# Gathering expert rows by plain f32 products, half a weight unit staged early, and four moves of small steps in a two-model transformer kernel

## The reference, cut to what matters

```python
def squared_relu_mlp(h, w1, w2):
    return jnp.square(jax.nn.relu(h @ w1)) @ w2

def ec_moe(h, w_router, w_gate, w_up, w_down):      # cap = 32 tokens of each expert
    logits = jnp.einsum('bsd,de->bse', h, w_router)
    aff = jax.nn.softmax(logits, axis=-1)
    top_val, top_idx = lax.top_k(aff.transpose(0, 2, 1), cap)
    xg = jax.vmap(lambda hb, ib: hb[ib])(h, top_idx)
    g = jnp.einsum('becd,edf->becf', xg, w_gate)
    u = jnp.einsum('becd,edf->becf', xg, w_up)
    y = jnp.einsum('becf,efd->becd', jax.nn.silu(g) * u, w_down) * top_val[..., None]
    return scatter_add(y, top_idx)
```

## Time and profile before

| | |
|---|---|
| median of 3 runs | 2306.1 us (2304.45 to 2307.54) |
| the profiled execution | 2316.15 us, span 2314.1 us |
| PE busy | 1975.1 us (85%), granted clock 0.94 in the mean |
| DVE, ACT busy | 913.9 us (39%), 621.4 us (27%) |
| DMA in the expert stretches | 426 GB/s, nine tenths busy or more in nearly every slice |

### The profile page before, as it was taken

How to read it: one execution, slowest core, us unless ns; L and a number is a source line. 1 busy time by engine, 2 the same in 40 slices (tenths; PEclk the granted TensorE clock), 3 DMA queues, 4 the chain that set the end, 5 groups by cost and what they waited for, 6 DMA issues and landing times.

```text
span 2314.1 us, 34736 instructions
## 1 busy us (share of the span) xinstructions
PE 1975.1 (85%) x14706; PEld 1371.2 (59%) x14706; DVE 913.9 (39%) x1636; ACT 621.4 (27%) x1067; POOL 32.9 (1%) x51
## 2 busy tenths in 40 slices
PE   8988999999998999999997666667999997666665
PEld 7776757888656887988854222223978854222222
DVE  4665645767554576544521000002544531000001
ACT  3332334431134443464410000001464420000000
POOL 0100000000000000000000000000000000000000
PEclk9999999999999999999999888878999999888888
DMA  9311125678863776542699999999642699999997
GB/s 326 126 38 39 39 82 216 250 263 294 306 230 133 253 256 223 183 145 104 245 403 424 426 426 426 426 426 408 222 141 90 244 409 426 426 426 426 427 427 314
DMA packets 150918, 641.93 MB, mean 277 GB/s; under 512 B 9406, under 2 KB 30936, under 8 KB 117654
## 3 DMA queue, kind: packets, MB, share of 16 engines
q1 hardware_dynamic: 144506, 637.13, 69.6%
q10 hardware_dynamic: 6300, 3.20, 0.5%
HBM read 639.21 MB, written 1.10 MB: 277 GB/s over the span
## 4 chain that ended last, share of the span: by engine, by line
PE 61%; DMA 29%; DVE 4%; ACT 3%; issue 2%; DVEq 1%; SPq 0%; POOL 0%; ACTq 0%; POOLq 0%
DMA ring<-in_w_down 29%; PE psum L1413 6%; PE psum L1028 5%; PE psum L1029 5%; PE psum L1030 5%; PE psum L1566 4%; PE psum L726 3%; PE psum L1132 3%; PE psum L1403 2%; PE psum L1541 2%; PE psum L1292 2%; PE psum L1291 2%; PE psum L1293 2%; PE psum L1149 1%; PE psum L797 1%
## 5 line engine op out<-in xcount | busy, mean ns | idle before, releaser
L1541 PE MATMUL psum<-ring,arena 128*32 128x256 f32 x3840 | 270.6, 434 | 156.8 <-DMA ring<-in_w_up 119.9
L1541 PEld LDWEIGHTS psum<-ring,arena 128*32 128x32 f32 x3840 | 135.1, 121 | 294.5 <-issue 129.5
L1566 PE MATMUL psum<-ring,arena 128*32 128x512 f32 x992 | 155.2, 759 | 79.9 <-DMA ring<-in_w_down 70.0
L1028 PE MATMUL psum<-arena_r 128*128 128x512 f32 x512 | 205.6, 402 | 12.2 <-DVE arena_r L2033 7.1
L2446 DVE TENSOR_TENSOR arena<-psum,arena 128x256 f32<-128x256 f32 x32 | 13.6, 425 | 501.9 <-PE psum L1541 501.9
L1030 PE MATMUL psum<-ring_r,arena_r 128*128 128x512 f32 x512 | 203.2, 397 | 0.0
L1701 DVE TENSOR_TENSOR ring_r<-ring,arena_r 128x2048 fp32r<-128x2048 f32 x64 | 143.7, 2288 | 86.9 <-ACT arena_r L2525 86.9
L2453 DVE TENSOR_TENSOR arena<-psum,arena 128x512 f32<-128x512 f32 x64 | 44.3, 692 | 249.6 <-PE psum L1566 248.0
L2525 ACT CAST arena_r<-ring 128x2048 fp32r<-128x2048 f32 x64 | 119.5, 1903 | 72.9 <-PE psum L1030 72.9
L2962 ACT ACTIVATE arena<-psum 128x256 f32<-128x256 f32 x32 | 12.3, 385 | 467.6 <-PE psum L1541 467.6
L1566 PEld LDWEIGHTS psum<-ring,arena 128*32 128x32 f32 x992 | 31.3, 125 | 171.5 <-DMA ring<-in_w_down 99.2
(11 more groups left out here) (429 smaller groups left out, 3348.5 us busy)
## 6 DMA issues: line engine op xcount, KB each, us to landing
ring<-in_w_down SPq DMA_DIRECT2D x62, 2048.0 KB, 26.1
ring<-in_w_gate SPq DMA_DIRECT2D x60, 2048.0 KB, 26.5
ring<-in_w_up SPq DMA_DIRECT2D x60, 2048.0 KB, 26.0
ring<-in_mlp_w SPq DMA_DIRECT2D x32, 2048.0 KB, 8.6
ring<-in_w_mod SPq DMA_DIRECT2D x24, 2048.0 KB, 11.1
ring<-in_w_in SPq DMA_DIRECT2D x20, 2048.0 KB, 8.2
ring<-in_gdn_w_in SPq DMA_DIRECT2D x8, 2048.0 KB, 13.8
ring<-in_dswa_w_in SPq DMA_DIRECT2D x9, 1536.0 KB, 13.2
```

The costliest lines, as they stand in the source:

```text
L1028: mm(o, xh, wh, start=start, stop=False, skip_group_check=True)
L1541: ins = mm(PS[32 * j:32 * j + 32, 4 + m, 0:T], XGF[:, k, 0:CAP] if first else XGE[:, k, :], row[:, j * T:(j + 1) * T], start=u == 0 and kk ...
L1566: ins = mm(PS[32 * j:32 * j + 32, (7, 4)[half], :], HTE[:, k % 2, 32 * (k // 2):32 * (k // 2) + 32], (next_row(4, j) if ahead else W(v + 4 ...
```

## The change

1. *Start.* PE no longer waits for the parameters first; it runs ten `keep_busy` products as soon as the zero tile is there.
2. *MLP.* `turn(0)` moves into `up(1,1)`, behind its second pair of rows. On ACT `square(0)` moves between the two halves of the down weights, ahead of `relu(1,1)`; on DVE `hidden_low(0)` moves between the two halves too.
3. *DSWA.* `mod_cols(7)` and its sum move from ahead of `out_steps(0)` to behind `weighted(5)`. Then come four steps of `out_steps(2)`, `mod_cols(8)`, and the other eight. On DVE `mod_sum(7)` stands directly ahead of `mod_sum(8)` and the two `low` of the next MLP.
4. *Router.* `keep_busy` products go between the transposes and the router products, whose order is cut finer.
5. *Gather.* `first_rows` and `gather` use the plain f32 rows XN and a plain f32 `ST`. The four parts are no longer made.
6. *Staging.* The room of `XNH_R` becomes `NEXT5`, half of expert 1's sixth unit. SP issues it, and two parts of `NEXT1`, between the up and the down units of expert 0. The ring's load of that unit shrinks to 1 MB.

```diff
-        XNH_R = ar_r[:, 0:TT * D].rearrange("p (t d) -> p t d", t=TT)
+        NEXT5 = ar[:, 0:2 * D]
...
+                    if between:
+                        between()
                     for u in range(max(first - 4, 0), 2):
-                        load(n + 4 + u, two(A["w_down_2"])[u * 512:(u + 1) * 512, :].rearrange("(j p r) n -> p j (r n)", p=P, r=2), turn)
+                        rows = two(A["w_down_2"])[u * 512 + (T if first else 0):(u + 1) * 512, :]
+                        load(n + 4 + u, rows.rearrange("(j p r) n -> p j (r n)", p=P, r=2), turn)
...
+                def free_rooms():
+                    sp.dma_start(NEXT5, down[512:512 + T, :].rearrange("(p r) n -> p (r n)", r=2)).then_inc(sem("next1_in"), 16)
+                    for part, ks in ((1, slice(6, 7)), (2, slice(7, 8))):
+                        sp.dma_start(NEXT1[part].rearrange("p (k n) -> p k n", n=D), second[:, ks, :]).then_inc(sem("next1_in"), 16)
+                expert(0, 0, 0, free_rooms)
...
-            pe.wait_ge(sem("params_in"), PARAMS)
             pe.wait_ge(sem("filled"), 1)
+            keep_busy(10, 0)
+            pe.wait_ge(sem("params_in"), PARAMS)
...
-                up(1, 1, 5)
-                turn(0)
+                up(1, 1, 5, lambda: turn(0))
...
-            mod_cols(7, 2)
-            pe.wait_ge(sem("mod_out"), 8)
+            pe.wait_ge(sem("mod_out"), 7)
             pe.wait_ge(sem("tok_out"), 6 + 4)
             out_steps(0, 0, 3)
...
             weighted(5)
+            mod_cols(7)
+            out_steps(2, 0, 4)
             mod_cols(8)
-            out_steps(2, 0, 12)
+            out_steps(2, 4, 12)
...
-                for t in range(TT):
-                    norm_split(L * 2 + 5, t, True)
-                    router(0, 6 * t, 6 + 2 * t)
+                keep_busy(2, 7)
+                norm_split(L * 2 + 5, 0, True)
+                keep_busy(2, 1)
+                router(0, 0, 2)
+                keep_busy(1, 1)
+                router(0, 2, 4)
+                keep_busy(1, 1)
+                norm_split(L * 2 + 5, 1, True)
+                router(0, 4, KC)
+                keep_busy(1, 1)
                 router(1, 0, KC).then_inc(sem("router_mm"), 1)
-                keep_busy(2, 1)
+                keep_busy(3, 1)
...
-                        for part in (XNH_R, XN_R):
-                            ins = mm(o, part[:, t, :].rearrange("p (q k) -> p k q", k=KC)[:, dc], ST_R[:, t, a:z],
-                                     start=t == 0 and part is XNH_R, stop=t == 1 and part is XN_R, skip_group_check=True)
+                        ins = mm(o, by_rows(t)[:, dc], ST[:, t, a:z], start=t == 0, stop=t == 1, skip_group_check=True)
...
+                    for t in range(TT):
+                        ins = mm(bank(5 + half), ST[:, t, 0:ROWS4], XN[:, t, half * 512:(half + 1) * 512], start=t == 0, stop=t == 1)
...
                 for u in range(NU):
-                    if u < NU - 1:
-                        low(l, down_unit(u))
-                    hidden_low(u)
+                    if u == 0:
+                        low(l, down_unit(0), (0,))
+                        hidden_low(0)
+                        low(l, down_unit(0), (1,))
...
-            mod_sum(7, 2)
...
             mod_unit(17)
+            mod_sum(7)
             mod_sum(8)
             low(1, 0)
...
-                high(l, down_unit(0))
+                high(l, down_unit(0), (0,))
+                square(0)
+                high(l, down_unit(0), (1,))
                 relu(1, 1)
-                square(0)
```

More of the change, by code:

```diff
@@ L389, in next_row @@
         def next_row(unit, kk):
+            if unit == 5:
+                return NEXT5[:, kk * D:(kk + 1) * D]
             if unit == 4:
@@ L554, in _, with expert @@
                     ld(V_OUT + u, halves(one(A["w_out_2"]), u))
-                def expert(e, first, ahead=AHEAD):
+                def expert(e, first, ahead=AHEAD, between=None):
                     n = u2 + V_MOE - ahead
@@ L564, in expert @@
                                 load(n + 2 * m + u, pmajor(two(A[name]))[:, 4 * u:4 * u + 4, :], turn)
+                    if between:
+                        between()
                     for u in range(max(first - 4, 0), 2):
-                        load(n + 4 + u, two(A["w_down_2"])[u * 512:(u + 1) * 512, :].rearrange("(j p r) n -> p j (r n)", p=P, r=2), turn)
+                        rows = two(A["w_down_2"])[u * 512 + (T if first else 0):(u + 1) * 512, :]
+                        load(n + 4 + u, rows.rearrange("(j p r) n -> p j (r n)", p=P, r=2), turn)
                 second = pmajor(one(A["w_gate_2"])[1])
                 sp.dma_start(NEXT2.rearrange("p (k n) -> p k n", n=D), pmajor(one(A["w_up_2"])[1])[:, 0:4, :]).then_inc(sem("next0_in"), 16)
-                expert(0, 0, 0)
+                down = one(A["w_down_2"])[1]
+                def free_rooms():
[3 more added lines that the diff above has]
+                expert(0, 0, 0, free_rooms)
                 sp.dma_start(NEXT0.rearrange("p (k n) -> p k n", n=D), second[:, 0:4, :]).then_inc(sem("next0_in"), 16)
-                for part, ks in ((1, slice(6, 7)), (2, slice(7, 8))):
-                    sp.dma_start(NEXT1[part].rearrange("p (k n) -> p k n", n=D), second[:, ks, :]).then_inc(sem("next1_in"), 16)
                 sp.wait_ge(sem("router_mm"), L + 1)
@@ L577, in _ @@
                 sp.wait_ge(sem("sel_mm"), L * 3 + 2)
-                down = one(A["w_down_2"])[1]
                 for part, room in enumerate((X[:].rearrange("p t d -> p (t d)"), NEXT4)):
@@ L1045, in up @@
                             ins = three(bank(b), HTH_R[:, k, ts], HT_R[:, k, ts], wh[:, c], wl[:, c], k == 0, k == KC - 1)
+                            if k == 1 and between:
+                                between()
                         if t == 1 and hf == 0:
@@ L1577, in expert @@
                     ins.then_inc(sem("expert_done"), 1)
-                def first_rows(half, part, t):
-                    return mm(bank(5 + half), ST_R[:, t, 0:ROWS4], part[:, t, half * 512:(half + 1) * 512],
-                              start=t == 0 and part is XNH_R, stop=t == 1 and part is XN_R, skip_group_check=True)
-                pe.wait_ge(sem("xn_hi"), L * 2 + 2)
-                pe.wait_ge(sem("st_ready"), L * 3 + 1)
+                pe.wait_ge(sem("st_ready"), L * 2 + 1)
                 for half in range(2):
@@ L1588, in _ @@
                         pe.wait_ge(sem("gr_out"), L * 2 + 2)
-                    first_rows(half, XNH_R, 0)
-                    first_rows(half, XN_R, 0)
-                    first_rows(half, XNH_R, 1)
-                pe.wait_ge(sem("st_ready"), L * 3 + 2)
-                for half in range(2):
-                    first_rows(half, XN_R, 1).then_inc(sem("xg_mm"), 1)
+                    for t in range(TT):
+                        ins = mm(bank(5 + half), ST[:, t, 0:ROWS4], XN[:, t, half * 512:(half + 1) * 512], start=t == 0, stop=t == 1)
+                    ins.then_inc(sem("xg_mm"), 1)
                 for half in range(2):
@@ L1693, in residual, with low @@
                         square_part(h)
-            def low(l, i):
-                for hf in range(2):
+            def low(l, i, hfs=(0, 1)):
+                for hf in hfs:
                     h, slot, at = 2 * i + hf, mlp_unit(l, i) % RING, slice(hf * HALF, (hf + 1) * HALF)
@@ L2035, in mlp @@
                 for u in range(NU):
-                    if u < NU - 1:
-                        low(l, down_unit(u))
-                    hidden_low(u)
+                    if u == 0:
+                        low(l, down_unit(0), (0,))
+                        hidden_low(0)
+                        low(l, down_unit(0), (1,))
+                    else:
+                        if u < NU - 1:
+                            low(l, down_unit(u))
+                        hidden_low(u)
                     if u < NU - 2:
@@ L2410, in _ @@
                 chosen(0, 4)
-                rows_low(1).then_inc(sem("st_ready"), 1)
                 def gathered(n, a, z, src):
@@ L2514, in norm, with high @@
                                  bias=0.0 if shift is None else shift(dc)).then_inc(sem("ht0_ready"), 1)
-            def high(l, i):
+            def high(l, i, hfs=(0, 1)):
                 full(act, mlp_unit(l, i))
-                for hf in range(2):
+                for hf in hfs:
                     h = 2 * i + hf
```

25 lines of the change are left out of this document (11 added, 14 removed).

## The result

The changed kernel takes 2294.8 us (median of 7 runs, 2290.3 to 2298.3) beside 2309.9 us for the kernel before on the same chip: a ratio of 0.993, 95% interval 0.9914 to 0.9946, or 12 to 20 us faster; the medians differ by 15.1 us. The forecast was 18.8 us. The profiled execution took 2290.3 us, the shortest of the seven, with a span of 2288.3. The two profiled executions differ by 25.9 us, almost eleven more than the medians, so a single pair of traces says too much; the table further down therefore sets fourteen traces side by side.

What follows compares the result with a forecast made beforehand. PE was taken to bound the kernel up to expert 0 of each layer, then the weight transfer. Terms 4.0 + 11.8 + 1.8 + 1.2 = 18.8 us; 2306.1 - 18.8 = 2287 us, range 2277 to 2299.

Steps and rivals of the forecast that it cites:

- The start: Ten zero products at the start bring transposes and decay products to the upper clock level: 4.0 us faster, ends 1.8 and 7.3.
- The MLPs: In both MLPs the wait before `down(0)` goes (3.5 us each) and the clock holds behind it: 11.8 us faster, lower end 7.1.
- The DSWA: Output products come 8.5 us better, 4.7 returned behind two sums, 2.0 to a new pause: 1.8 us faster, between 0 and 3.8.
- Router and first rows: Before expert 0, `first_rows` costs 1.6 us more and the router's clock gains 1.6: 0 a layer, between +1.3 and -4.6.
- Rival A: The clock falls in the router anyway, each layer losing 4.6 us: 2296 us, chance 0.14.
- Gather and staging: In the experts, 2.46 us fewer bytes a layer against a gather 4.2 us longer: -0.2 and +1.4, 1.2 us faster in sum.
- the hole: DMA dips some 60 us after the steady transfer begins, standing 2.7 and 1.1 us because of the longer gather.
- the forecast's own signs: Listed signs of right or wrong; wrong included waits elsewhere in the MLPs, a router at 0.50, or DMA that never dips.
- D: `gather` in the experts runs at the lower clock level, 24.0 us long: 5.3 us slower, 2311 us, chance 0.04.
- Rival C: The MLPs' waits come back because what moves behind the square makes the next weights late: 2294 us, chance 0.08.

Runs made afterwards that it cites:

- e2: The kernel before with only the ten zero products at the start added: 1.0013 of before, 2311.7 us.
- e0: The changed kernel run again unaltered, for a second profile: 0.9936 of before, 2295.1 us.
- e5: The changed kernel without the ten zero products at the start: 0.9933 of before, 2295.5 us.
- e1: The kernel before with only the MLPs' new order: 0.9955 of before, 2301.4 us.
- e6: The changed kernel with the second MLP's first low half on DVE moved between the two modulation sums: 0.9918 of before, 2291.3 us.
- e12: e11 with the router as in the kernel before, without zero products between its groups: 0.9922 of before, 2292.6 us.
- e11: The changed kernel with e6's move and the start's zero products as 128 records instead of 20: 0.9894 of before, 2287.3 us.
- e3: The kernel before with only the seventh set of modulation columns in the DSWA moved later: 0.9992 of before, 2310.0 us.
- e9: The changed kernel with many more short zero products at the start, meant as 128 records but shifting by 240: 0.9965 of before, 2301.1 us.

## Why the prediction was right, and where it was not

The time, the direction and most steps came out. Two terms were off, the start by some 4 us and the gather with the staging by some 3, in opposite directions, and nearly cancelled. That the sum fits so well is luck.

- **The start: 4.0 us, measured none.** This step failed. The local part was right: products at the upper level, chunk products from 15.3 instead of 20.15, 4.8 us on average at the first turn pause (70.8 us in the six kernels with 20 zero records, 75.6 in the five without). What the step left out is that twenty records more shift all that PE executes later against the blocks in which its instructions come. The forecast asked what the zero products delay and what they speed up, and did not ask what they move. The core is 5.4 us longer with them in the mean of the same kernels (221.6 and 216.2 us; 6.8 in e2 against before, 5.6 in e0 against e5): 3.0 us more of pauses, and a clock that is at the lower level for 17.1 to 23.9 us instead of 10.2 (20.5 in e3).
- **The MLPs: 11.8 us, measured 10.4 alone (6 to 15 by its interval) and 5.5 + 5.5 to 6.7 by stage.** Right with its parts, the wait and the clock behind it.
- **The DSWA: 1.8 us, measured 1.8 alone, in an interval that holds none, and 0 to 2.6 by stage.** Each part was right: the output products come 5.7 us sooner and run at 2.81 us, the low halves are behind two sums, the new pause is 3.76 us (3.6), and the second MLP starts at the lower level. Against e1, which has all of the MLPs' gain and no such pause, the second MLP takes 2.7 us more (2.0 were taken off). e6 shows that pause and clock have one cause: move the one line, and 5.2 us come back in the two stages.
- **Router and first rows: 0 a layer, measured 0 within a us.** The two parts of it are shown as well: without the zeros (e12 against e11) the clock falls for 10.2 and 6.8 us instead of 3.4 and 3.4, and expert 0 comes 3.2 and 0.8 us later (1.6 each were forecast). Rival A, the fall in the router, did not come in layer 0 of the changed kernel; in layer 1 it came for 3.4 us, and expert 0 was no later for it.
- **Gather and staging: 1.2 us, measured 3.9 alone, 4.4 by stage** (439.0 and 440.2 us in the mean of the four kernels without it, 436.7 and 438.1 in the eight with it and one gather). The bytes are worth what was said, the hole that was to eat them is the step that failed in size. By the forecast's own signs a DMA that never dips speaks against it, and it does not dip. In hand were 1.4 and 1.1 us, where the forecast came to 2.7 and 1.1 too few. The gather took 11.2 us and not 12.0, so 3.4 more and not 4.2; DMA moved 420 GB/s in that stretch and not 426, which is 0.9 us over 64. And in layer 0 the profiled execution before had its clock down behind the old gather, so that the load came 59.9 us behind the first, where e1, e2 and e3 have it at 58.6. That is 3.0 of the 4.1 us in layer 0 and 1.7 of 2.2 in layer 1; the rest stays open.
- **D, the gather at the lower level**, did not come: 1.00 throughout. Rival C fell with e1.

The eleven us by which the profiled pair exceeds the medians are in no term: the core and the expert stretches differ by some us between executions, also of one kernel (e0 and the first profile: 440.7 and 435.3 in the first layer's experts). In the core it is the time at the lower clock, as the stage table shows; why that differs with the same records (e11 and e12) stays open. In e0's experts the weights fall behind in the first 45 us of the steady transfer: its first load is issued 2.1 us later than in the first profile and lands 2.0 later, but from 1204 on they land some 5 us later, to the end. What held them up stays open too.

## What to carry to other kernels

Work that only keeps PE busy is not free because it lies in a wait: count its records, since in stretches of very short products it moves the places where PE runs out of instructions. A whole period of records leaves them where they were (e11, e12), if the added products do not themselves outrun the supply (e9). When an operation is moved later, look at the queue behind its consumer and put something useful between two waits; the move is worth its full gain only then. Take the room that a transfer has in hand from more than one execution, or measure it by doubling what it hides.

## What the runs showed of the hardware

- PE's records of 32x32 products come in blocks of 128 (127 of them in the trace), with pauses of 0.2 to 2.2 us between them that the profile puts down to issue; each of the 121 in the cores ends 1.2 to 1.7 us after a packet of 16384 bytes has landed on the queue that the page calls "instruction". Inserting 20, 110 + 18 or 240 records moves them by just that number, modulo 128. At the start, PE took 207 records of such products in 1.93 us and then stood 3.34 us (e9).
- At the very start the column of the granted clock says 1.00 in four of the five kernels without zeros, while the decay products take 0.219 us a record, twice that of the changed kernel (0.117). The traces of these four hold no record of the clock before 24 to 25 us, and the column shows 1.00 where there is none: there the pace is to be read.
- Shortening a pause from 3.76 to 0.84 us gave 5.2 us in its two stages, 2.9 of waiting and 2.3 of clock behind it (e6 against the changed kernel).
